# Row order for the three bf16 parts of the second norm, read with a step of eight by the expert gather

## What is computed

```
h = rmsnorm(x, norm_ffn_g)                       # 512 x 1024
group = argmax(h @ w_grp + b_grp)                # 4 groups
two experts of 8 inside the group, softmax weights
for e in range(32):
    hid = silu(h @ w_gate[e]) * (h @ w_up[e])    # 1024 -> 512
    y  += combine[:, e:e+1] * (hid @ w_down[e])  # 512 -> 1024
out = rmsnorm(x + y, final_norm_g)
```

## Time and profile before

| | |
|---|---|
| three timed runs | 804.3, 806.95, 808.2 us; median 806.95 |
| span of the profiled execution | 804.1 us |
| TensorE busy (matmul) | 746.0 us, 93% |
| TensorE weight loads busy | 383.9 us, 48% |
| DVE, ACT, POOL busy | 224.4, 148.7, 77.7 us |
| TensorE's mean granted clock | 0.980 of full speed |

### The profile page before, as it was taken

One profiled execution on the slowest core, in us unless ns is written; L12 is line 12 of the kernel. 1 busy time (PEld: TensorE's weight loads), 2 busy tenths in 40 slices (PEclk: granted clock), 3 DMA queues, 4 the chain that ended last, 5 costly groups with the idle time before them and its releaser, 6 DMA issues.

```text
span 804.1 us, 13704 instructions
## 1 busy us (share of the span) xinstructions
PE 746.0 (93%) x6202; PEld 383.9 (48%) x6202; DVE 224.4 (28%) x444; ACT 148.7 (18%) x308; POOL 77.7 (10%) x70
## 2 busy tenths in 40 slices
PE   5999999999899997999999999999999889988960
PEld 4444454464555467456545455544545454444520
DVE  3017862003566166311111111111111111111126
ACT  5153230033355263100000000000000000000004
POOL 0632200000000022000000000000000000000002
PEclk9999999999999998999999999999999999999995
DMA  9431130410630648799999999999999999999955
GB/s 327 107 104 45 61 106 1 157 60 1 263 156 1 242 176 315 272 401 423 427 425 421 424 428 422 422 428 421 425 425 425 422 426 423 423 425 425 406 208 205
DMA packets 35244, 234.72 MB, mean 292 GB/s; under 512 B 5730, under 2 KB 7138, under 8 KB 18928
## 3 DMA queue, kind: packets, MB, share of 16 engines
q1 hardware_dynamic: 32624, 229.61, 70.1%
q0 software_dynamic: 2560, 4.20, 1.4%
HBM read 227.50 MB, written 10.49 MB: 296 GB/s over the span
## 4 chain that ended last, share of the span: by engine, by line
PE 74%; DMA 20%; DVE 3%; ACT 2%; issue 1%; DVEq 0%; POOLq 0%; SPq 0%
PE bank L471 21%; DMA arena<-in_w_up 19%; PE bank L772 18%; PE bank L795 9%; PE bank L755 7%; PE bank L640 4%; PE bank L685 3%; PE bank L774 1%; PE bank L775 1%; PE bank L595 1%; PE bank L674 1%; PE bank L658 1%; PE bank L784 1%; PE bank L455 1%; DVE arena L1303 1%
## 5 line engine op out<-in xcount | busy, mean ns | idle before, releaser
L772 PE MATMUL bank<-arena 128*64 128x512 f32 x928 | 206.3, 597 | 14.7 <-DMA arena<-in_w_up 13.8
L471 PE MATMUL bank<-arena 128*128 128x512 f32 x384 | 167.0, 594 | 0.0
L772 PEld LDWEIGHTS bank<-arena 128*64 128x64 f32 x928 | 70.6, 138 | 146.6 <-issue 145.7
L1094 DVE TENSOR_TENSOR arena<-bank,arena 128x512 f32<-128x512 f32 (+1 forms) x96 | 47.7, 511 | 308.0 <-ACT arena L1053 216.1
L795 PE MATMUL bank<-arena 128*64 128x512 f32 x512 | 116.9, 598 | 0.5 <-ACT arena L1057 0.5
L471 PEld LDWEIGHTS bank<-arena 128*128 128x128 f32 x384 | 72.3, 190 | 89.8 <-issue 89.5
L755 PEld LDWEIGHTS bank<-arena 128*128 128x128 bf16 x3072 | 95.9, 98 | 24.4 <-issue 23.9
L755 PE MATMUL bank<-arena 128*128 128x64 bf16 x3072 | 100.2, 193 | 0.0
L1053 ACT ACTIVATE arena<-bank 128x256 f32<-128x256 f32 x32 | 12.3, 384 | 358.8 <-PE bank L772 324.8
L1504 POOL DMA_INDIRECT y_tok<-arena x32 | 31.3, 977 | 436.0 <-DVE arena L1383 408.1
L795 PEld LDWEIGHTS bank<-arena 128*64 128x64 f32 x512 | 33.9, 136 | 57.1 <-issue 54.8
(11 more groups left out here) (163 smaller groups left out, 479.7 us busy)
## 6 DMA issues: line engine op xcount, KB each, us to landing
arena<-in_w_gate SPq DMA_DIRECT2D x31, 2048.0 KB, 28.6
arena<-in_w_down SPq DMA_DIRECT2D x31, 2048.0 KB, 31.6
arena<-in_w_up SPq DMA_DIRECT2D x30, 2048.0 KB, 28.4
arena<-in_w_in SPq DMA_DIRECT2D x6, 2048.0 KB, 8.0
arena<-y_tok SPq DMA_DIRECT2D x8, 512.0 KB, 5.3
arena<-in_x SPq DMA_DIRECT2D x4, 512.0 KB, 5.9
arena<-in_w_out SPq DMA_DIRECT2D x2, 1024.0 KB, 8.1
arena<-in_w_out SPq DMA_DIRECT2D x1, 2048.0 KB, 18.4
```

The source lines that it names most:

```text
L471: m = pe.matmul(pbank[unit_bank(n)][:], lhs(k), rhs(k), start=(k == 0), stop=(k == KC - 1))
L772: mm = pe.matmul(both, xT[:, k], gate_and_up(e, k, cols), start=(k == 0), stop=(k == KC - 1))
L1094: return nc.vector.tensor_tensor(out_, a, b, op)
```

## The change

The three parts are stored in row order. `hi`, `rest`, `mid` and POOL's subtraction now work on plain rows, with whole rows or contiguous halves of 512; `x1_by_chunk` is gone, and with it the 32-byte step. The gather's view `h2_part` is made from those rows by `"p (q k) -> p k q"`: its chunk `k` is every eighth bf16 value, a step of 16 bytes. No instruction is added, removed or moved on any engine; only access patterns differ.

```diff
-        rest2 = [at(128 + 4 * i, KC, P) for i in range(2)]
+        rest2 = [at(128 + 4 * i, D) for i in range(2)]
...
-        h2_part = [[at(179 + 6 * t + 2 * i, D // 2).bitcast(BF16).rearrange("p (k q) -> p k q", k=KC) for i in range(3)]
-                   for t in range(TT)]
+        h2_row = [[at(179 + 6 * t + 2 * i, D // 2).bitcast(BF16) for i in range(3)] for t in range(TT)]
+        h2_part = [[row.rearrange("p (q k) -> p k q", k=KC) for row in rows] for rows in h2_row]
...
-        def x1_by_chunk(t):
-            return x1[:, t].rearrange("p (q k) -> p k q", k=KC)
-
         halves = [slice(0, KC // 2), slice(KC // 2, KC)]
-        all_k = slice(0, KC)
+        row_halves = [slice(0, D // 2), slice(D // 2, D)]
+        all_row = slice(0, D)
...
-                nc.scalar.activation(h2_part[t][0][:, ks], x1_by_chunk(t)[:, ks], ACT.Identity,
+                nc.scalar.activation(h2_row[t][0][:, ds], x1[:, t, ds], ACT.Identity,
                                      scale=rstd2[:, t:t + 1]).then_inc(hi_done, 1)
...
-                nc.scalar.copy(h2_part[t][1][:, ks], rest2[t % 2][:, ks]).then_inc(mid_done, 1)
+                nc.scalar.copy(h2_row[t][1][:, ds], rest2[t % 2][:, ds]).then_inc(mid_done, 1)
...
-                nc.vector.scalar_tensor_tensor(rest2[t % 2][:, ks], x1_by_chunk(t)[:, ks], rstd2[:, t:t + 1],
-                                               h2_part[t][0][:, ks], ALU.mult, ALU.subtract).then_inc(rest_done, 1)
+                nc.vector.scalar_tensor_tensor(rest2[t % 2][:, ds], x1[:, t, ds], rstd2[:, t:t + 1],
+                                               h2_row[t][0][:, ds], ALU.mult, ALU.subtract).then_inc(rest_done, 1)
...
-                nc.gpsimd.tensor_tensor(h2_part[t][2], rest2[t % 2], h2_part[t][1], ALU.subtract).then_inc(parts_done, 1)
+                nc.gpsimd.tensor_tensor(h2_row[t][2], rest2[t % 2], h2_row[t][1], ALU.subtract).then_inc(parts_done, 1)
```

More of the change, by code:

```diff
@@ L1012, in x1_T_evict, with hi, mid @@
                 nc.scalar.copy(hT2[t % 2][:, 0:4].rearrange("p a b -> p (a b)"), pbank[4][:]).then_inc(h2T_act, 1)
-            def hi(t, ks):
+            def hi(t, ds):
                 act.wait_ge(sumsq_done, TT + t + 1)
                 act.wait_ge(rstd_done, TT + t + 1)
-                nc.scalar.activation(h2_part[t][0][:, ks], x1_by_chunk(t)[:, ks], ACT.Identity,
+                nc.scalar.activation(h2_row[t][0][:, ds], x1[:, t, ds], ACT.Identity,
                                      scale=rstd2[:, t:t + 1]).then_inc(hi_done, 1)
-            def mid(t, ks, rests):
+            def mid(t, ds, rests):
                 act.wait_ge(rest_done, rests)
-                nc.scalar.copy(h2_part[t][1][:, ks], rest2[t % 2][:, ks]).then_inc(mid_done, 1)
+                nc.scalar.copy(h2_row[t][1][:, ds], rest2[t % 2][:, ds]).then_inc(mid_done, 1)
             square(0)
@@ L1027, in _ @@
             x1_T_evict(0)
-            hi(0, all_k)
+            hi(0, all_row)
             square_root(1)
             x1_T_evict(1)
-            hi(1, all_k)
-            mid(0, all_k, 1)
-            mid(1, all_k, 2)
+            hi(1, all_row)
+            mid(0, all_row, 1)
+            mid(1, all_row, 2)
             square(2)
             square_root(2)
-            hi(2, all_k)
+            hi(2, all_row)
             x1_T_evict(2)
@@ L1040, in _ @@
             square_root(3)
[L1041 to L1045, removed]
+            hi(3, row_halves[0])
+            mid(2, all_row, 3)
+            hi(3, row_halves[1])
+            mid(3, row_halves[0], 4)
+            mid(3, row_halves[1], 5)
             act.wait_ge(cdiff_done, 1)
@@ L1296, in x1_T_evict, with rest @@
                 nc.vector.tensor_copy(hT2[t % 2][:, 4:8].rearrange("p a b -> p (a b)"), pbank[5][:]).then_inc(h2T_vec, 1)
-            def rest(t, ks, his):
+            def rest(t, ds, his):
                 dve.wait_ge(rstd_done, TT + t + 1)
@@ L1310, in _ @@
             norm2(1)
-            rest(0, all_k, 1)
+            rest(0, all_row, 1)
             x1_T_evict(1)
-            rest(1, all_k, 2)
+            rest(1, all_row, 2)
             residual(2)
@@ L1319, in _ @@
             norm2(3)
-            rest(2, all_k, 3)
+            rest(2, all_row, 3)
             x1_T_evict(3)
-            rest(3, halves[0], 4)
-            rest(3, halves[1], 5)
+            rest(3, row_halves[0], 4)
+            rest(3, row_halves[1], 5)
             route(2, 4)
@@ L1493, in _ @@
                 pool.wait_ge(mid_done, t + 1)
-                nc.gpsimd.tensor_tensor(h2_part[t][2], rest2[t % 2], h2_part[t][1], ALU.subtract).then_inc(parts_done, 1)
+                nc.gpsimd.tensor_tensor(h2_row[t][2], rest2[t % 2], h2_row[t][1], ALU.subtract).then_inc(parts_done, 1)
             for h in range(2):
                 pool.wait_ge(mid_done, TT + h)
-                nc.gpsimd.tensor_tensor(h2_part[TT - 1][2][:, halves[h]], rest2[(TT - 1) % 2][:, halves[h]],
-                                        h2_part[TT - 1][1][:, halves[h]], ALU.subtract).then_inc(parts_done, 1)
+                nc.gpsimd.tensor_tensor(h2_row[TT - 1][2][:, row_halves[h]], rest2[(TT - 1) % 2][:, row_halves[h]],
+                                        h2_row[TT - 1][1][:, row_halves[h]], ALU.subtract).then_inc(parts_done, 1)
             last_row = EXPERTS * SLOTS - 1
```

## The result

The changed kernel takes 882.53 us (880.47 to 883.93, 4 runs), the kernel before 805.95 (804.3 to 808.2, 4 runs, the three shown above among them): a ratio of 1.0943, 95% interval 1.0925 to 1.0961, 9.4% slower. The profiled execution has a span of 879.6 us where the one before had 804.1. Two executions further down, one of `e1_gather_alone` at 1352.26 us and one of `e2_norm_alone` at 1573.59, were in a slower state: the ratios leave them out, the medians given there (884.23 and 805.33) count them and would be 884.06 and 805.08 without.

What follows compares the result with a forecast made beforehand. TensorE bounds the experts early, `in_w_up` transfers from about 562 to 745.61 us. Span 804.1 + 91.2 gather - 15.0 waits - 1.5 norm = 878.8, plus 2.85 to timed runs: 882 us, range 803 to 908.

Steps and rivals of the forecast that it cites:

- The price of a load: Gather weight loads: about 1.87 ns per new 16-byte piece, taking a pair from 30.7 to 60 ns.
- Four streams: Gather's bf16 loads: four columns go at a time, so each stream has 32 of 128 pieces, 60 ns.
- The gather's growth: All gathers on TensorE: 2.8 us for the first, 2.85 for each of 31 others, 91.2 us in all.
- The waits: Expert stage: TensorE's waits, 15.0 us in all, vanish as its work per expert exceeds the transfers' 15.42 us.
- the norm: Second norm: contiguous reads on ACT and DVE give 1.5 us back, between 0.8 and 2.6.
- The rule that spoke against it: Skill text on SBUF: two hits a line are free, 8 bf16 a free stride; gather would stay at 30.7 ns.
- The hidden load: Rival, 16 in 100: flat 0.51 ns a stepped column, gather load 30 ns, hidden under the matmul; 805.5 us.
- One stream: Rival, 9 in 100: stepped gather loads lose four-at-a-time reading, 122 to 240 ns a pair; 1071 to 1433 us.
- The falling clock: Rival, 8 in 100: longer gather drops TensorE's granted clock to half in each expert; 932 to 988 us.
- the likeliest case: Whole kernel: pairs of 50 ns and more, four streams, full clock; 858 to 903 us, 57 in 100.
- The stepped load's record: Gather weight load in the profile: fixed 84 plus streamed 60, near 144 ns instead of 98.
- the lower bound: Gather: L471's 106 ns as two passes gives 1.66 ns a piece, 53 ns a pair, 69 us; 860 us total.

Runs made afterwards that it cites:

- e1_gather_alone: Kernel before with only the gather's weight loads read at the 16-byte step, norm as before: 884.23 us, ratio 1.0948.
- e2_norm_alone: Changed kernel with the gather reading contiguous chunks again, norm as changed: 805.33 us, ratio 0.998.
- the sweep: Kernel before plus, behind the last `down`, 64 pairs of weight load and matmul per column step, width and type: 980.57 us; main groups rerun with warming matmuls: 869.57 us.
- the 8-byte step: Changed kernel with parts stored as two groups of four chunks, gather step 4 bf16: 805.84 us, ratio 0.9997 against the kernel before.
- the 4-byte kernel: Changed kernel with parts stored as four groups of two chunks, gather step 2 bf16: 805.95 us, ratio 0.9992 against the kernel before.

## Why the prediction was right

**The price of a load** was the step on which all rested, and it held: 60 ns forecast for a pair, 61.9 (5.94 / 96 and 4.46 / 72) and 59.6 (1.43 / 24) measured. It came from three rows with other steps, other engines and other types (L784, ACT's and DVE's reads of `x1`), put into one law by pieces of 16 bytes, and the sweep bears the law out between 8 and 16 bytes, within 4 ns, and at two widths.

**Four streams** was an inference from the 14 ns that a contiguous bf16 load streams. The sweep shows it: 128 pieces cost 62 ns in a bf16 load of 128 columns and 233 in a float32 one, and a bf16 load of half the columns takes twice as long.

**The sum.** The gather's growth was put at 91.2 us and is 2.98 + 31 x (2.25 + 0.73) = 95.4. The waits gave their 15.0, and the norm 1.4 where 1.5 was said. That makes +79.0, and the spans differ by 75.5. The rest is known in kind: the earlier trace rows show a `gate_up` of 7.10 us behind a wait where it is 6.87 without, some 2.1 us in nine waits; the one behind the tenth took 8.78 at a clock of 0.81, 1.9 more; against it, 0.7 us, by which the stages ahead of the norm ended later in this execution. So a wait cost more than its length, and the 15.0 us were worth 19; this term was mis-sized. The forecast of 882 thus came from a gather 4 us too short and a saving at the waits that I had counted too low by about as much; that it hit within 1 us is luck on top of a sum with the right terms.

**The rule that spoke against it.** In the Trainium skill, Advanced Engine Details and Errata, SBUF Cachelines, two hits on a line give full performance. TensorE's bf16 loads pay already at two hits (step 4: 33 ns against 25 to 27 at steps of 1 to 3); what the page says of a line for each access, a penalty, does hold. The sentence in the Trainium skill, SBUF — State Buffer, Door 1, that 8 bf16 are a free stride doesn't hold here: 62 ns against 27.

**The rivals.** The hidden load fell with the first run: a price of 0.51 ns for any stepped column would have given 30 ns at all steps. One stream fell for 128 columns and is what happens at 64. The falling clock did not come with the change: it was seen behind the gather once, in another kernel, for 1.5 us, and the one fall inside the expert stage of the kernel before (1.9 us) is gone in the changed one. The range was wide because of these; the likeliest case's own, 858 to 903, held.

**What was read wrongly.** The stepped load's record was to be 84 + 60 = 144 ns and is 171 in the median, 142 at the least. The 84 ns that are fixed for contiguous loads aren't for stepped ones, or a part of the record is waiting; no run settles which. The DMA share was to be 0.93 and is 0.98, at 387 GB/s for 423. The first gather was to start 0.8 to 2.6 us earlier than 318.29 and starts 0.7 earlier, at 317.57, since the stages ahead of the norm ended 0.7 later. The pace in the chain was the safe measure. And the lower bound, two passes of a float32 load over its pieces, rested on a picture that the sweep contradicts; as a bound it did no harm. The last router was to become the norm's next bound, and in the changed kernel it didn't: the chain stays on DVE, as before. It passed through the router only in the profile of the 8-byte step, where its 16 matmuls took 3.23 us at a clock of 0.56.

## What to carry to other kernels

Count the 16-byte pieces that an operand touches before changing a layout, and count them at the reader that reads most often: here five reads each on ACT and DVE lost a step and 3072 weight loads got one. A load's growth is free only while it stays under the matmul it hides behind (29 ns here, passed at a step of 8 bytes with 33 to 35) and, beyond that, while the waits of its engine last (15 us here, worth 17 to 19 with what ended with them). Where two users want opposite orders, a short step can serve both, if the instructions that make it don't multiply: 4 bytes left the gather at its pace, 8 cost it 4 ns a pair. Here neither won anything in time.

## What the runs showed that was not expected

- bf16 weight loads of 64 columns with a step take about twice as long as loads of 128 columns: 61 against 33 ns at 8 bytes, 120 against 62 at 16. Nothing in the kernel itself had shown a price by width.
- The pace of a stepped load is the same at either clock: 62 ns at 0.50, 59 at 1.00.
- A second DVE instruction in half a row of `rest`, 256 elements each, can cost far more than their length when GpSimd works beside them: 3.12 us for the last two of the 4-byte kernel, where one of 512 took 2.03 in the changed kernel, also beside GpSimd, and 0.66 to 0.74 without company. That GpSimd is the cause wasn't tested apart.
